# GpSimd's low parts of the down weights in four operations of 256 elements

## What is computed

```python
def merge_and_ffn(x, y_ssm, y_attn, g_ssm, g_attn, w_ssm_out, w_attn_out, w_o, norm2_g, w_up, w_down):
    mix = jax.nn.sigmoid(g_ssm) * (y_ssm @ w_ssm_out) + jax.nn.sigmoid(g_attn) * (y_attn @ w_attn_out)
    x = x + mix @ w_o
    h = rms_norm(x, norm2_g)
    return x + jnp.square(jax.nn.relu(h @ w_up)) @ w_down
```

## Time and profile before

| | |
|---|---|
| median of three runs | 1793.41 us |
| profiled execution, whole | 1793.14 us |
| its span, first to last instruction | 1791.3 us |
| mean granted TensorE clock | 0.975 |
| TensorE matmuls busy | 1652.7 us (92%) |
| VectorE busy | 1154.9 us (64%) |
| ScalarE busy | 737.6 us (41%) |
| GpSimd busy | 695.4 us (39%), 435 instructions |
| low_d on GpSimd (L3156) | 147.0 us, 56 instructions, from 1428.4 us on |

### The profile page before, as it was taken

One profiled execution on the slowest core, in us unless ns is written; L12 is line 12 of the kernel. 1 busy time (PEld: TensorE's weight loads), 2 busy tenths in 40 slices (PEclk: granted clock), 3 DMA queues, 4 the chain that ended last, 5 costly groups with the idle time before them and its releaser, 6 DMA issues.

```text
span 1791.3 us, 31523 instructions
## 1 busy us (share of the span) xinstructions
PE 1652.7 (92%) x12434; PEld 1525.3 (85%) x12448; DVE 1154.9 (64%) x1864; ACT 737.6 (41%) x1333; POOL 695.4 (39%) x435
## 2 busy tenths in 40 slices
PE   6999879978999989787799999899999989999998
PEld 6997559978999955555499998899999989999998
DVE  5774676998855537564244138765555578998896
ACT  6423546547334435443322335444444433333342
POOL 7111118774111100000445331344444477677682
PEclk9999989989999999999899999999999989999999
DMA  5322161213961114003552433464544475454422
GB/s 160 107 79 59 37 66 52 92 53 100 169 171 64 40 58 143 1 1 120 173 177 96 153 103 95 144 198 145 178 147 145 145 246 168 157 169 132 145 86 98
DMA packets 170198, 209.13 MB, mean 117 GB/s; under 512 B 27410, under 2 KB 114418, under 8 KB 170002
## 3 DMA queue, kind: packets, MB, share of 16 engines
q1 hardware_dynamic: 170050, 207.10, 38.3%
HBM read 148.28 MB, written 58.78 MB: 116 GB/s over the span
## 4 chain that ended last, share of the span: by engine, by line
PE 32%; POOL 8%; DVE 4%; DMA 3%; issue 2%; ACT 2%; SPq 1%; DVEq 0%; ACTq 0%; POOLq 0%
PE psum L139 10%; PE psum L141 10%; PE psum L140 10%; POOL da_lo L3156 4%; DMA view_at<-hid_dram 2%; POOL view_at L3165 1%; ACT da_hi L3032 1%; POOL view_at L3172 1%; POOL view_at L3175 1%; DVE view_at L3236 1%; POOL view_at L3168 1%; DVE b_lo L3242 1%; SPq L2618 0%; DVE view_at L3367 0%; PE psum L2757 0%
## 5 line engine op out<-in xcount | busy, mean ns | idle before, releaser
L139 PE MATMUL psum<-db_hi,da_hi 128*128 128x264 f32 x896 | 257.0, 287 | 11.6 <-DVE view_at L3352 8.1
L139 PE MATMUL psum<-b_hi,ua_hi 128*128 128x264 f32 x896 | 256.7, 287 | 11.1 <-DVE psum L3300 3.8
L140 PE MATMUL psum<-db_lo,da_hi 128*128 128x264 f32 x896 | 257.3, 287 | 0.0
L141 PE MATMUL psum<-db_hi,da_lo 128*128 128x264 f32 x896 | 257.2, 287 | 0.0
L141 PE MATMUL psum<-b_hi,ua_lo 128*128 128x264 f32 x896 | 255.4, 285 | 0.0
L140 PE MATMUL psum<-b_lo,ua_hi 128*128 128x264 f32 x896 | 255.1, 285 | 0.0
L139 PE MATMUL psum<-h_hi,w_hi 128*128 128x352 f32 x600 | 197.1, 329 | 19.5 <-POOL w_lo L211 19.5
L3152 POOL TENSOR_TENSOR ua_lo<-view_at,ua_hi 128x512 fp32r<-128x512 f32 x99 | 137.3, 1392 | 190.0 <-ACT ua_hi L2961 189.9
L140 PE MATMUL psum<-h_lo,w_hi 128*128 128x352 f32 x600 | 194.4, 324 | 0.0
L141 PE MATMUL psum<-h_hi,w_lo 128*128 128x352 f32 x600 | 194.2, 324 | 0.0
L211 POOL TENSOR_TENSOR w_lo<-view_at,w_hi 128x2048 fp32r<-128x2048 f32 (+1 forms) x18 | 81.1, 4505 | 280.6 <-ACT w_hi L205 280.5
(11 more groups left out here) (395 smaller groups left out, 4053.6 us busy)
## 6 DMA issues: line engine op xcount, KB each, us to landing
hid_dram<-view_at SPq DMA_DIRECT2D x112, 264.0 KB, 2.2
view_at<-hid_dram SPq DMA_DIRECT2D x56, 528.0 KB, 3.9
view_at<-w_in SPq DMA_DIRECT2D x18, 1024.0 KB, 5.6
view_at<-w_up SPq DMA_DIRECT2D x16, 1024.0 KB, 6.0
view_at<-w_down SPq DMA_DIRECT2D x32, 512.0 KB, 6.2
gate_dram<-view_at SPq DMA_DIRECT2D x48, 176.0 KB, 2.0
view_at<-gate_dram SPq DMA_DIRECT2D x16, 528.0 KB, 4.4
view_at<-cache_k SPq DMA_DIRECT2D x32, 256.0 KB, 3.1
```

The source lines that it names most:

```text
L139: nc.tensor.matmul(out, lhs[0], rhs[0], start=start, stop=False, skip_group_check=more)
L140: nc.tensor.matmul(out, lhs[0], rhs[1], start=False, stop=False, skip_group_check=more)
L141: return nc.tensor.matmul(out, lhs[1], rhs[0], start=False, stop=stop, skip_group_check=more)
```

## The change

low_d on GpSimd computes the same 128 x 1024 low part. Before, one instruction covered it. Now there are four, one for each of the two rows of 512 and each half of it, 128 x 256 each. Only the first has the wait on da_hi ahead of it, and only the last raises da_lo. Everything else is as it was.

```diff
             def low_d(n):
                 pool.wait_ge(da_hi, n + 1)
-                tt(dal[n % SLOTS], src_d(n), f32(dah[n % SLOTS]), ALU.subtract).then_inc(da_lo, 1)
+                for k in range(2):
+                    for z in range(2):
+                        at_ = (slice(None), k, slice(EH // 2 * z, EH // 2 * (z + 1)))
+                        ins = tt(dal[n % SLOTS][at_], src_d(n)[at_], f32(dah[n % SLOTS])[at_], ALU.subtract)
+                ins.then_inc(da_lo, 1)
```

## The result

Four runs of the changed kernel have a median of 1823.15 us (1821.49 to 1826.97), the kernel before 1793.79 us over four runs; the ratio is 1.0176 with a 95% interval of 1.0155 to 1.0197. The change costs 29 us. The forecast was 1830.

A forecast was written before the change was run, and what follows sets the result against it. A closed chain of GpSimd, SyncE, transfer and ScalarE bounds the down projection; six passes growing 4.6 + 1.2 = 5.8 give 35, less 1 of lead: 1793 + 34 + 2 (clock) + 1 (end) = 1830 us, range 1809 to 1842.

The forecast's parts named there:

- The bound: Down projection: GpSimd's low_d and sums, SyncE's in-order queue, transfer and ScalarE form a closed chain, 42.4 us against TensorE's 41.1.
- Length of the parts: GpSimd's low_d: four parts take 3.17 us, 0.76 us more per low_d, six per block in the waiting chain: 4.6 us.
- a pass: One trip of the waiting chain over a block of down weights, 42.4 us, repeated six times; forecast to grow 5.8 us.
- the gap of 0.08: Pause read behind a 240-element GpSimd subtraction: 0.70 us long, next start 0.78 behind; parts taken as 0.81 start to start.
- Collisions: GpSimd against VectorE in the down projection: VectorE gets in between parts, +1.2 us per block, bounds -1 to 2.5.
- Lead, clock, end: Down projection: TensorE's 1 us lead subtracted, 2 us for half clock after the last stall, 1 us for late last additions.
- Stalls of 4 to 7 us at every border: Down projection: TensorE stalls once per block, 4 to 7 us, with clock 0.5 behind it.
- 1 (cheap parts): GpSimd's low_d: fixed time overlaps and VectorE's shorter waits cost nothing more; 3.1 us per block, 1812 us; chance 0.14.
- 2 (hidden): GpSimd's low_d: its extra 43 us go into its 97.6 us of idle time; 1793 us; chance 0.06.
- 3 (faster by VectorE's shorter waits): Down projection: VectorE waits less behind short parts, drains come earlier, TensorE's stalls of 8.1 and 2.5 shrink; 1788 us; chance 0.05.
- 4 (everything collides): Down projection: each low_d loses to VectorE at a seam, blocks 6 and 7 become GpSimd-bound; 1848 us; chance 0.09.
- The estimate of 0.2 us a low_d: GpSimd's low_d: skill page's price leaves about 60 ns fixed time; three more operations cost 0.2 us, 1.1 per block.

## Why the prediction was right, and where its terms were off

- **The bound.** Right. A closed ring of GpSimd, SyncE, transfer and ScalarE, slower than TensorE and not visible in the table of busy shares. The changed order of SyncE, which shortens no operation, takes away all 29 us; the low_d outside the ring is free within 2 us. That SyncE waits for the fourth sum and not for db_lo(7d + 4) held too: in the pass shown above they end 37.0 and 25.8 us behind the block's first db_hi (38 and 25 forecast).
- **Length of the parts.** Too high: 0.76 us a low_d, 4.6 a pass; measured 0.41 (2.82 against 2.41), 2.5 a pass. I had added the gap of 0.08 of the earlier trace rows to each part. In low_d each part starts about 0.70 us after the one ahead ((2.83 - 0.74) / 3), a little before that one's record of 0.74 ends; even my lower bound of 0.5 was too high. The gap was read from another line's operations and called that of every unsynchronised one; these have none.
- **Collisions.** Too low: +1.2 a pass; measured low_d 6 x (0.69 - 0.23) = 2.8, less 0.5 that the sums save (91.4 us before, 87.3 after), so 2.3. It is within the bounds given (up to 2.5) and was the term with the weakest ground: all that GpSimd loses to VectorE is now 7 x 0.69 + 1.4 on the sums = 6.2 us a block, more than the 5.6 that I had taken for the most it could meet. That the forecast came within 7 us is in part luck: one term was 2.1 us too high and the other 1.1 too low. Together they are 5.8 forecast and 4.8 measured, and six times 1.0 is nearly the whole miss.
- **Lead, clock, end.** -1 + 2 + 1 = 2 forecast, 1.5 measured from the db_hi of block 6 on. Here the chain differs from the forecast: block 6 takes GpSimd 38.0 us, as forecast, but with the lead gone the chain stays on it through blocks 6 and 7 until 1792.
- **Stalls of 4 to 7 us at every border.** In half of the cases: they are 4.1, 0.5, 8.1, 4.5, 6.0 and 1.3 us. Passes are not alike, since collisions come in whole units of 1.03 or 0.47 us.
- **Rivals.** 1 (cheap parts) had the length nearly right (0.5 us a low_d against 0.41) and missed the collisions. 2 (hidden) is true only with the pass open. 3 (faster by VectorE's shorter waits) named a real gain: db_lo's median fell from 2.05 to 1.61 us and the first stall by 3. Here it only lengthens the lead, as forecast; with the ring open it may show, by some 2 us. 4 (everything collides) forecast 8 us a pass and 8 at the end, and it takes eight parts to come near that: 10.0 and 10. The estimate of 0.2 us a low_d, worked out from the Trainium skill (GPSIMD Engine Reference, section "Elementwise — side-by-side cycle accounting"), was nearer for the length (0.41) than the price that I took, but it has no collisions in it, and its sum of 1799 is 24 us off.

## What to carry to other kernels

Ask of a longer operation on a half-idle engine whether that engine waits inside a ring: follow the chain of waits around one period and compare the period with the bound engine's own pace. If the ring closes through an in-order queue, a prefetch issued a little later can open it, and here that took away the whole loss without making any operation shorter. Splitting an operation that takes turns with another engine's costs twice, for the seams and for the other engine getting in at them; it can help where that engine's wait is what the rest stands on.

## What the runs showed of the hardware

A GpSimd subtraction with two SBUF inputs costs 0.14 us for each further part, whatever the number (2.41, 2.55, 2.82, 3.38 us for 1, 2, 4, 8 parts). VectorE's operations with two SBUF inputs take turns with it instruction by instruction: GpSimd loses whole steps of about 1.03 us (1056 elements; 3.86 against 2.83 us) or 0.47 us (528; 3.29 against 2.82), and with db_lo cut to 64 elements an undivided low_d is back at 2.41 us. So the more seams, the more often VectorE is let in: 0.23, 0.49, 0.69 and 0.97 us a low_d.
